# Feed-forward layers whose first two units run on operands without the norm, and two successive norms computed in one round

## The reference

```
def rmsnorm(x, g):
    y = x * lax.rsqrt(jnp.mean(x * x, axis=-1, keepdims=True) + RMS_EPS)
    return y * g
def modulate(h, shift, scale):
    return h * (1 + scale[:, None, :]) + shift[:, None, :]
def swiglu(h, w13, w2):                      # ffn2 to ffn5
    a, b = jnp.split(h @ w13, 2, axis=-1)
    return (jax.nn.silu(a) * b) @ w2
def conv_glu_ffn(h, w_up, conv_w, conv_b, w_down):   # ffn0, ffn1, ffn6
    z = h @ w_up
    z = conv_w[0] * z2 + conv_w[1] * z1 + conv_w[2] * z + conv_b   # z1, z2: z one and two tokens back
    gate, val = jnp.split(z, 2, axis=-1)
    return (jax.nn.silu(gate) * val) @ w_down
```

## Time and profile before

| what | us |
|---|---|
| median of 3 runs | 2327.18 (2322.79 to 2336.35) |
| the profiled execution | 2330.64 |
| its span on the core | 2328.8 |
| PE busy | 2237.0 (96%) |
| DVE busy | 1436.0 (62%) |
| ACT busy | 1165.8 (50%) |
| POOL busy | 508.9 (22%) |

### The profile page before, as it was taken

One profiled execution on the slowest core, in us unless ns is written; L12 is line 12 of the kernel. 1 busy time (PEld: TensorE's weight loads), 2 busy tenths in 40 slices (PEclk: granted clock), 3 DMA queues, 4 the chain that ended last, 5 costly groups with the idle time before them and its releaser, 6 DMA issues.

```text
span 2328.8 us, 45915 instructions
## 1 busy us (share of the span) xinstructions
PE 2237.0 (96%) x18384; PEld 2152.7 (92%) x18384; DVE 1436.0 (62%) x1989; ACT 1165.8 (50%) x1587; POOL 508.9 (22%) x257
## 2 busy tenths in 40 slices
...
GB/s 250 98 46 1 37 217 316 305 185 163 82 281 306 270 143 332 312 271 166 89 211 307 341 187 203 189 187 145 83 189 180 198 165 145 145 169 160 180 195 93
DMA packets 63374, 439.07 MB, mean 189 GB/s; under 512 B 6887, under 2 KB 9480, under 8 KB 10778
## 3 DMA queue, kind: packets, MB, share of 16 engines
...
## 4 chain that ended last, share of the span: by engine, by line
PE 66%; DVE 18%; issue 9%; ACT 4%; POOL 1%; DMA 1%; DVEq 1%; SPq 0%; ACTq 0%; POOLq 0%
PE ps L283 15%; PE ps L284 15%; PE ps L285 15%; DVE mix L587 10%; DVE w_lo L268 3%; PE ps L400 1%; PE ps L411 1%; ACT w_hi L262 1%; PE ps L297 1%; PE ps L299 1%; PE ps L305 1%; PE ps L1402 1%; DVE gf L710 1%; DVE acc L698 1%; DMA mix<-in_modw 1%
## 5 line engine op out<-in xcount | busy, mean ns | idle before, releaser
L283 PE MATMUL ps<-h_hi,w_hi 128*128 128x256 f32 x3544 | 991.0, 280 | 7.0 <-DVE w_lo L268 3.7
L284 PE MATMUL ps<-h_lo,w_hi 128*128 128x256 f32 x3544 | 985.6, 278 | 0.0
L285 PE MATMUL ps<-h_hi,w_lo 128*128 128x256 f32 x3544 | 985.4, 278 | 0.0
L268 DVE TENSOR_TENSOR w_lo<-ring,w_hi 128x2048 fp32r<-128x2048 f32 x273 | 625.3, 2292 | 497.8 <-ACT w_hi L262 489.4
L262 ACT ACTIVATE w_hi<-ring 128x2048 fp32r<-128x2048 f32 x335 | 640.6, 1914 | 132.8 <-PE ps L285 126.5
L283 PEld LDWEIGHTS ps<-h_hi,w_hi 128*128 128x128 f32 x3544 | 669.2, 189 | 14.8 <-issue 9.3
L284 PEld LDWEIGHTS ps<-h_lo,w_hi 128*128 128x128 f32 x3544 | 671.1, 189 | 0.2
L285 PEld LDWEIGHTS ps<-h_hi,w_lo 128*128 128x128 f32 x3544 | 669.1, 189 | 0.0
L283 PE MATMUL ps<-g_hi,w_hi 128*128 (+1 forms) x1232 | 344.8, 280 | 16.2 <-DVE g_lo L720 12.8
L284 PE MATMUL ps<-g_lo,w_hi 128*128 (+1 forms) x1232 | 343.3, 279 | 0.0
L285 PE MATMUL ps<-g_hi,w_lo 128*128 (+1 forms) x1232 | 343.1, 279 | 0.0
...
## 6 DMA issues: line engine op xcount, KB each, us to landing
...
```

Source lines behind the costliest of these rows:

```text
L268: dve.tensor_tensor(w_lo[:, n % SLOTS], ring[:, n % SLOTS], w_hi[:, n % SLOTS], ALU.subtract).then_inc(lo_ready[n % SLOTS], 1)
L283: pe.matmul(o, w[0], a_hi, start=first, stop=False, **kw)
L284: pe.matmul(o, w[0], a_lo, start=False, stop=False, **kw)
L285: return pe.matmul(o, w[1], a_hi, start=False, stop=last, **kw)
```

## The change

All seven feed-forward layers become "late" (`LATE`). The norm's factor of a token, 1/rms, is the same for all channels, so it may be put on the result of a product instead of on its operand. In a late layer:

- ACT writes `s_hi`, x times the gain, as each piece of the residual comes, and DVE, between the pieces, `s_lo`; PE runs units b and b+1 on these, into banks 2 to 5 (`late_pe`). Where the layer has a shift, two more columns of the operand carry it (258 instead of 256), so that its product comes out beside the others in a column of its own.
- The sum of squares runs on PE between unit b and unit b+1, from three blocks (POOL adds two more times to bring six blocks into one); root and reciprocal follow, and PE spreads the factor after a quarter of unit b+1. From there `hf`, `h_hi` and `h_lo` are made as before, for the units from b+2 on. The two results on hand are multiplied by the factor when they are evicted, by DVE (`scaled`, which waits for a copy of the factor, `rstd`, that ACT makes).
- `keep_warm` is gone from these norms.
- The weights' low parts move: DVE does `lo` of b+1 and b+2 ahead of the reciprocal; POOL does those of b+3 and b+4, which DVE did before inside m = 0 and m = 1; and where a feed-forward layer is followed by a late one (ffn1 and ffn3), POOL does `lo` of its unit b at the end of the layer before, where DVE did it in halves.
- fin1 has no round of its own: ffn2 takes the product of both gains as its gain, PE sums x squared with weights 1 and final gain squared (16 matmuls), and the factors of both norms come out of the two sums. x itself is multiplied by fin1's gain and factor later, in four steps inside ffn2 (`late_dve_rescale`). fin2 and fin3 stay as they are.

The core of the diff:

```diff
+        def late_act_squares(act, tag, gain, ready):
+            if shifted_at[tag] is not None:
+                a = shifted_at[tag]
+                act.wait_ge(*after(f"dve:mod{a // 72}"))
+                act.activation(s_hi[:, :, T], mod[:, a:a + 8], ACT.Copy)
+                act.activation(s_hi[:, :, T + 1], mod[:, a:a + 8], ACT.Copy).then_inc(*step(f"act:{tag}.shift"))
+            for q, (k, n) in enumerate(square_tiles(tag, KD)):
+                act.wait_ge(*ready(q)[0])
+                for j in range(k, k + n):
+                    act.activation(s_hi[:, j, 0:T], x[:, j], ACT.Identity,
+                                   scale=gain(j)).then_inc(*step(f"act:{tag}.s{j}"))
+                act.activation(hf[:, k:k + n], x[:, k:k + n], ACT.Square).then_inc(*step(f"act:{tag}.sq{q}"))
+                if q == 0:
+                    act.activation(root[:, 2:3], eps_at[1e-6], ACT.Sqrt)
...
+        def late_act(act, tag, gain, shift, ready):
+            b = late_first(tag)
+            late_act_squares(act, tag, gain, ready)
+            hi(act, b + 2)
+            if tag in FUSED:
+                act.wait_ge(*after(f"dve:{tag}.var"))
+                act.activation(root[:, 0:2], fold[:, 2:4], ACT.Sqrt, scale=1.0 / D).then_inc(*step(f"act:{tag}.rms"))
+                act.activation(fold[:, 4:6], late_sums(tag, 0), ACT.Sqrt, scale=1.0 / D,
+                               bias=eps_at[1e-6]).then_inc(*step(f"act:{tag}.rms1"))
+            else:
+                norm_act_root(act, tag, D, 1e-6)
+            hi(act, b + 3)
+            norm_act_parts(act, tag, KD, shift)
+            act.activation(rstd[:], ps[7][:, 0:T], ACT.Copy).then_inc(*step(f"act:{tag}.over"))
+            hi(act, b + 4)
...
+        def late_pe(pe, tag):
+            b, cols, two_banks = late_first(tag), late_columns(tag), shifted_at[tag] is not None
+            s = b % SLOTS
+            pe.wait_ge(lo_ready[s], b // SLOTS + 1)
+            if two_banks:
+                pe.wait_ge(*after(f"dve:{stage_ahead(tag)}.res1"))
+            for k in range(KD):
+                pe.wait_ge(*after(f"act:{tag}.s{k}"))
+                for blk in range(2):
+                    c, o = (2 * k + blk) * P, late_out(tag, 0, blk)
+                    pe.matmul(o, w_hi[:, s, c:c + P], s_hi[:, k, 0:cols], start=k == 0 and (two_banks or blk == 0),
+                              stop=False, skip_group_check=True)
+                    pe.matmul(o, w_lo[:, s, c:c + P], s_hi[:, k, 0:cols], start=False, stop=False, skip_group_check=True)
+            for k in range(KD):
+                pe.wait_ge(*after(f"dve:{tag}.s{k}"))
+                for blk in range(2):
+                    c = (2 * k + blk) * P
+                    done = pe.matmul(late_out(tag, 0, blk), w_hi[:, s, c:c + P], s_lo[:, k, 0:cols], start=False,
+                                     stop=k == KD - 1 and (two_banks or blk == 1), skip_group_check=True)
+            done.then_inc(unit_done, 1)
...
+                for k, w in ((6, "act:{}.sq3"), (7, "act:{}.sq4"), (0, "pool:{}.sum")):
+                    pe.wait_ge(*after(w.format(tag)))
+                    for c in range(NCH):
+                        done = pe.matmul(ps[0][:, c:c + 1], hf[:, k, c * P:(c + 1) * P], ones[:, 0:1],
+                                         start=k == 6 and c == 0, stop=k == 0 and c == 1, skip_group_check=True)
+            done.then_inc(*step(f"pe:{tag}.ss"))
+            n, s = b + 1, (b + 1) % SLOTS
+            pe.wait_ge(lo_ready[s], n // SLOTS + 1)
+            for blk in range(2):
+                for k in range(KD):
+                    c = (2 * k + blk) * P
+                    done = product(pe, late_out(tag, 1, blk), (w_hi[:, s, c:c + P], w_lo[:, s, c:c + P]), s_hi[:, k, 0:cols],
+                                   s_lo[:, k, 0:cols], k == 0 and (two_banks or blk == 0),
+                                   k == KD - 1 and (two_banks or blk == 1), skip_group_check=True)
+                    if blk == 0 and k == 3:
+                        late_pe_over(pe, tag)
...
+        def late_dve_lows(dve, tag, gain, q):
+            k, n = square_tiles(tag, KD)[q]
+            if q == 0 and shifted_at[tag] is not None:
+                a = shifted_at[tag]
+                dve.wait_ge(*after(f"act:{tag}.shift"))
+                for col in (T, T + 1):
+                    dve.tensor_tensor(s_lo[:, :, col], mod[:, a:a + 8], s_hi[:, :, col], ALU.subtract)
+            for j in range(k, k + n):
+                dve.wait_ge(*after(f"act:{tag}.s{j}"))
+                dve.scalar_tensor_tensor(out=s_lo[:, j, 0:T], in0=x[:, j], scalar=gain(j), in1=s_hi[:, j, 0:T],
+                                         op0=ALU.mult, op1=ALU.subtract).then_inc(*step(f"dve:{tag}.s{j}"))
...
+        def late_dve(dve, tag, gain, shift):
+            b = late_first(tag)
+            lo(dve, b + 1)
+            lo(dve, b + 2)
...
+            norm_dve_root(dve, tag)
+            norm_dve_parts(dve, tag, x, KD, gain, shift)
...
+        def late_dve_rescale(dve, tag, j):
+            for k in (2 * j, 2 * j + 1):
+                done = dve.scalar_tensor_tensor(out=x[:, k], in0=x[:, k], scalar=V(fin_gain[tag], k), in1=ps[7][:, T:2 * T],
+                                                op0=ALU.mult, op1=ALU.mult)
...
+        def late_pool(pool, tag):
+            b = late_first(tag)
+            if tag not in FUSED:
+                norm_pool(pool, tag)
+                pool.wait_ge(*after(f"pool:{tag}.pair1"))
+                pool.tensor_tensor(hf[:, 0], hf[:, 0], hf[:, 2], ALU.add).then_inc(*step(f"pool:{tag}.four"))
+                pool.wait_ge(*after(f"pool:{tag}.four"))
+                pool.tensor_tensor(hf[:, 0], hf[:, 0], hf[:, 4], ALU.add).then_inc(*step(f"pool:{tag}.sum"))
+            lo(pool, b + 3)
+            lo(pool, b + 4)
...
-        def residual_dve(dve, tag, last_unit, factor=None, between=None):
+        def residual_dve(dve, tag, last_unit, factor=None, between=None, lows=None):
             for q, (k, n) in enumerate(square_tiles(tag, KD)):
                 if q == 1 and between is not None:
                     lo_half(dve, between, 0)
+                if q > 1 and lows is not None:
+                    lows(q - 2)
...
-            return n if n < UNITS else None
+            return n if n < UNITS and not next_late(s) else None
...
+            def scaled(m):
+                dve.wait_ge(unit_done, BASE[name] + m + 1)
+                over = rstd[:]
+                dve.wait_ge(*after(f"act:{name}.over"))
+                if conv:
+                    for half in range(2):
+                        done = dve.tensor_tensor(zs[:, m, half], late_out(name, m, half), over, ALU.mult)
+                    done.then_inc(*step(f"dve:{name}.z{m}"))
+                    return
+                if 22 * f + m >= 2:
+                    dve.wait_ge(glo_done, 22 * f + m - 1)
+                for half in range(2):
+                    dve.tensor_scalar(fold[:, 8 + 2 * m + half:9 + 2 * m + half], late_out(name, m, half)[:, T:T + 1], 1.0, None,
+                                      ALU.mult)
+                dve.tensor_tensor(sil[:, m], late_out(name, m, 0)[:, 0:T], over, ALU.mult).then_inc(*step(f"dve:{name}.z{m}"))
+                dve.tensor_tensor(gf[:, m], late_out(name, m, 1)[:, 0:T], over, ALU.mult).then_inc(*step(f"dve:{name}.v{m}"))
...
-                if m % 2 == 0:
+                if m % 2 == 0 and m >= 2:
...
+                if name in FUSED and m in (2, 3, KF - 2, KF - 1) and isinstance(i, int):
+                    late_dve_rescale(dve, name, m - 2 if m < 4 else m - KF + 4)
...
+                    if s.startswith("ffn") and next_late(s):
+                        lo(pool, last_unit[s] + 1)
```

152 lines of the change are left out of this document (135 added, 17 removed).

## The result

| | before | after |
|---|---|---|
| median of 8 runs | 2335.14 us (2313.90 to 2338.45) | 2344.32 us (2340.05 to 2347.20) |
| span of the profiled execution | 2328.8 | 2341.0 |

The ratio is 1.0059, with a 95% interval of 1.003 to 1.0087: the changed kernel is 0.6% slower, some 14 us (the two medians alone differ by 9). The forecast was 2348 us, slower. It stood on a median of 2327.18 us for three runs of the kernel before; of eight runs that median is 2335.14. As a ratio the forecast was 1.009, just above the interval. The profiled executions differ by 12.2 us; the walk gave 21.

A forecast was written before the change was run, and what follows sets the result against it. It took PE, busy 2237 of 2328.8 us, as the bound, with DVE beside it in ffn0's loop. Terms 8.0 + 13.6 - 0.7 = +21 on 2330.64 gave 2351.6, less 3.5 for the runs' median: 2348 us, range 2304 to 2366.

The forecast's parts named there:

- The walk: Estimated timeline of PE, DVE, ACT and POOL at the late norms, worked through for ffn5; all layers' terms sum to +21 us.
- likeliest case: POOL's w_lo holds every form of DVE operation with two SBUF inputs: 2348 us, own range 2336 to 2360, chance 0.42.
- One of its own signs of being wrong: The prediction called itself wrong if PE's wait within unit b is under 1 us.
- ffn3 to ffn5, +8.0: Norms ahead of ffn3, ffn4 and ffn5: each +2.7 us from unit b to the end of b+3.
- The wait in unit b: Norms of ffn3 to ffn5: PE needs the last s_hi at 3.2 us, it comes at 5.9; 2.7 us lost.
- The wait for `h_lo`: Norms of ffn3 to ffn5: PE wants the last h_lo pair at 20.8 us, gets it at 24.0; waits 3.3.
- a rival alone: Slower and the clock falls too, behind PE's waits without keep_warm at late norms: up to 15 us more, 2363, chance 0.12.
- ffn0, ffn1, ffn6, +13.6: Conv layers: POOL's lo(b+4) holds DVE's first taps, the down unit starts at 28.9 us; +5.2, +3.2 and +5.2 us.
- +4.4 for ffn1's end: End of ffn1: POOL's new lo(b) for ffn2 starts 0.3 us ahead of DVE's g_lo, which goes 4.4 us later.
- ffn2 with fin1, -5.1: Start of ffn2: the 14.66 us lost at fin1 with ffn2 fall to about 9.5, held h_lo included.
- SCALAR_TENSOR_TENSOR free of the hold: Shifted h_lo and taps on DVE go on beside POOL's w_lo: -3 us in all, 2324, chance 0.20.
- The "no holding" rival: POOL's two w_lo lie in gaps of DVE at the late norms: -27 us, 2300, chance 0.26.

The follow-up runs named there:

- experiment 1: Changed kernel, but in ffn2 to ffn5 DVE, not POOL, does the low parts of b+3 and b+4; ratio to the kernel before 1.0030, median 2336.55 us.
- experiment 2: Changed kernel, but DVE in two halves, not POOL, does unit b's low part for ffn2 and ffn4; ratio to before 1.0032, median 2340.54 us.
- experiment 4: Changed kernel, but in ffn2 to ffn5 POOL starts b+4's low part only after DVE's last h_lo; ratio to before 1.0058, median 2350.00 us.
- experiment 6: Changed kernel with only ffn2 to ffn5 late, and DVE doing their low parts of b, b+3 and b+4; ratio to before 0.9952, median 2321.79 us.

## Why the prediction was right, and where its terms were off

Sign, place and mechanism were right: POOL's `w_lo` and DVE's operations with two SBUF operands hold each other, one instruction long, and experiments 1, 2 and 4 take the hold away and the waits with it. The time lies 4 us under the forecast, inside the likeliest case's own range. That it is so near is in part luck: the median of before turned out 8 us higher with more runs, and the walk's +21 was some 14 by the ratio and 12 by the profiles. One of its own signs of being wrong came true as well: PE's wait within unit b stayed under 1 us in ffn3 and ffn5, and only in ffn4 was it more. Term by term:

- **ffn3 to ffn5, +8.0.** Measured +5.5, but not the same +2.7 in each: +0.9, +2.5 and +2.2. The wait in unit b was to be 2.7; unit b took 6.28 us (1688.96 to 1695.24), 0.8 more than its length. In ffn3 it took 6.06. The last `s_hi` was out 3.7 us behind the mark and not 5.9: DVE's `s_lo` and POOL's sums hold each other less than I charged, and the eight `s_lo` took 4.8 us in all. The wait for `h_lo` was to be 3.3 and was 2.0 to 2.4. Against this two terms were missing: DVE's held `mod` operation at the end of ffn3, 2.2 us of wait ahead of ffn4 and 1.3 within its first unit, and the low clock in ffn5, 1.5. I had put the clock into a rival alone.
- **ffn0, ffn1, ffn6, +13.6 and +4.4 for ffn1's end.** The down unit was to start at 28.9 and did at 28.5 and 28.6 in ffn0 and ffn1; the loops of these two were +5.4 and +4.8. ffn1's whole +7.6 is its 3.2 and 4.4 together. ffn6, +5.2 in the walk, is +0.3 in these profiles; it ran at the long pace before and at the short one after. At the short pace on both sides (experiment 6 for the layer not late) it is 192.5 against 185.8 us from its first unit to its end, +6.7, but not as the walk had it. DVE is not at its bound in ffn6's loop (68.71 of 140 us busy, in the window of before above), and PE's turns show no lag: those behind the first take 16.32 us, as in the layer not late. The 6.7 are 2.0 ahead of the down unit, 1.7 in the first turn at a granted clock of 0.91, and 2.9 behind the loop.
- **ffn2 with fin1, -5.1.** The step that was off most: -8.6, when the 5.8 of the pace in its loop are taken out. I charged it with held `h_lo` as in ffn5, 3.3 us; PE never waits for `h_lo` there. DVE and POOL in ffn2's norm:

```profile
844.55 3.25 DVE L630 SCALAR_TENSOR_TENSOR h_lo<-hf,mod,h_hi 128x256 fp32r<-128x256 f32 x8
...
840.04 4.59 POOL L273 TENSOR_TENSOR w_lo<-ring,w_hi 128x2048 fp32r<-128x2048 f32 x1 [19.65 <-ACT w_hi L267]
847.82 4.62 POOL L273 TENSOR_TENSOR w_lo<-ring,w_hi 128x2048 fp32r<-128x2048 f32 x1 [3.18 <-ACT w_hi L267]
```

  The first `w_lo` ends as `h_lo` begins and the second begins as it ends. And DVE does not have two thirds of its time free in ffn2's loop, as the walk says from ffn4's: it is busy for 121.65 of 140 us there. The rescaling cost PE no wait all the same.
- **The pace** was in no term. It gave +5.8 in ffn2 and up to 3.1 in ffn0 and took about 5.8 in ffn6, so the sum of these two profiles partly hides it. Its sign could not be had from the trace of before.
- **The rivals.** SCALAR_TENSOR_TENSOR free of the hold is out (4.78 and 3.03 us for single operations). The "no holding" rival is true of ffn2 alone. The row that spoke for the former, a longest tap of 667 ns, was no evidence: in the trace of before no tap runs beside a `w_lo` of POOL, in ffn6 neither.

The Trainium skill's rule ("SBUF — State Buffer", section "Who interferes with whom") that the one issued first has the shared pair for its whole instruction agrees with this trace: 0.19 us of head start cost DVE 4.2 us, and in four pieces no hold was over 1.1 us.

What stays open: why a stage runs at the one or the other pace, and so how much of the 14 us is pace. The mixers vary too, with the same code: from the span's start to ffn0 the six profiles with ffn0 not late have 289.7 to 300.2 us, and the two profiles of before differ by 5.7 us in the stretch from ffn0's loop to ffn1. The waits in the table have their causes in the trace, but the time could not be split by cause.
